# Norms that add the squares of a group on VectorE and multiply the sum once by ones on TensorE

## What is computed

```python
def rmsnorm(x, w):
    xf = x.astype(jnp.float32)
    y = xf * lax.rsqrt(jnp.mean(xf * xf, axis=-1, keepdims=True) + RMS_EPS)
    return (y * w.astype(jnp.float32)).astype(x.dtype)
```

## Time and profile before

| | |
|---|---|
| median of 3 runs | 3441.77 us |
| lowest and highest | 3435.27 and 3444.86 us |
| profiled execution, its own time | 3437.32 us |
| its span in the trace | 3435.5 us |
| TensorE, matmuls busy | 2918.2 us (85%) |
| VectorE busy | 2044.2 us (60%) |
| ScalarE busy | 882.5 us (26%) |
| GpSimd busy | 740.4 us (22%) |

### The profile page before, as it was taken

The page is one execution under the profiler, slowest core; times in us unless marked ns, Lnnn a source line. Parts: engine busy times, 40 slices in busy tenths (PEclk is TensorE's granted clock), DMA queues, the critical chain, the costliest instruction groups (busy, mean ns, idle before and its releaser), DMA issues. The chain is left out here.

```text
span 3435.5 us, 45234 instructions
## 1 busy us (share of the span) xinstructions
PE 2918.2 (85%) x15875; PEld 2538.4 (74%) x15875; DVE 2044.2 (60%) x3475; ACT 882.5 (26%) x1371; POOL 740.4 (22%) x501
## 2 busy tenths in 40 slices
PE   4888896989778699989898999999967865789987
PEld 2666674779566479988887999999965733568865
DVE  2777645334434337998867778888854255355532
ACT  1222112023111113433333333333321033133201
POOL 0333200000000005655453322222200000034400
PEclk7888898999889899999999999999988976899998
DMA  1111112211122225687879999999942100033230
GB/s 56 50 37 43 55 55 73 74 50 49 49 72 75 69 86 169 214 254 242 254 242 293 391 339 347 345 347 346 347 141 95 49 0 18 31 104 98 67 122 37
DMA packets 264492, 496.99 MB, mean 145 GB/s; under 512 B 118834, under 2 KB 171442, under 8 KB 262467
## 3 DMA queue, kind: packets, MB, share of 16 engines
q1 hardware_dynamic: 209090, 336.24, 29.6%
q0 software_dynamic: 36864, 134.23, 10.8%
q10 hardware_dynamic: 18432, 25.17, 2.0%
HBM read 443.14 MB, written 52.43 MB: 144 GB/s over the span
## 5 line engine op out<-in xcount | busy, mean ns | idle before, releaser
L238 PE MATMUL banks<-hb_high,experts_high 128*128 128x384 f32 x1024 | 363.6, 355 | 46.4 <-POOL experts_low L1403 34.4
L239 PE MATMUL banks<-hb_low,experts_high 128*128 128x384 f32 x1024 | 352.6, 344 | 0.0
L240 PE MATMUL banks<-hb_high,experts_low 128*128 128x384 f32 x1024 | 352.2, 344 | 0.0
L238 PE MATMUL banks<-experts_ah,experts_high 128*128 128x384 f32 x1024 | 343.1, 335 | 5.4 <-DVE experts_al L1568 5.4
L239 PE MATMUL banks<-experts_al,experts_high 128*128 128x384 f32 x1024 | 343.0, 335 | 0.0
L240 PE MATMUL banks<-experts_ah,experts_low 128*128 128x384 f32 x1024 | 343.0, 335 | 0.0
L1403 POOL TENSOR_TENSOR experts_low<-experts_raw,experts_high 128x1024 fp32r<-128x1024 f32 x94 | 227.3, 2419 | 344.5 <-ACT experts_high L1312 344.4
L238 PEld LDWEIGHTS banks<-hb_high,experts_high 128*128 128x128 f32 x1024 | 199.7, 195 | 52.7 <-POOL experts_low L1403 39.5
L1312 ACT ACTIVATE experts_high<-experts_raw 128x1024 fp32r<-128x1024 f32 x128 | 135.6, 1059 | 353.8 <-PE banks L240 238.3
L1370 ACT ACTIVATE experts_high<-experts_raw 128x1024 fp32r<-128x1024 f32 x128 | 135.7, 1060 | 340.3 <-PE banks L240 340.3
L1565 DVE TENSOR_TENSOR experts_low<-experts_raw,experts_high 128x1024 fp32r<-128x1024 f32 x128 | 156.9, 1225 | 102.8 <-ACT experts_high L1370 102.8
(11 more groups left out here) (489 smaller groups left out, 7087.2 us busy)
## 6 DMA issues: line engine op xcount, KB each, us to landing
experts_raw<-in_u SPq DMA_DIRECT2D x128, 512.0 KB, 5.6
experts_raw<-in_v SPq DMA_DIRECT2D x128, 512.0 KB, 5.8
early_experts<-experts_A ACTq DMA_DIRECT2D x128, 192.0 KB, 4.5
expert_weights<-shared SPq DMA_DIRECT2D x48, 512.0 KB, 8.2
shared<-expert_weights SPq DMA_DIRECT2D x128, 192.0 KB, 5.5
shared<-early_experts SPq DMA_DIRECT2D x128, 192.0 KB, 6.2
up_raw<-in_w_up SPq DMA_DIRECT2D x44, 512.0 KB, 3.4
ssd_raw_w<-in_w_xbc SPq DMA_DIRECT2D x26, 512.0 KB, 3.4
```

Of the source, the lines that this page charges most:

```text
L238: nc.tensor.matmul(to, w[0], x[0], start=start, stop=False)
L239: nc.tensor.matmul(to, w[0], x[1], start=False, stop=False)
L240: return nc.tensor.matmul(to, w[1], x[0], start=False, stop=stop)
```

## The change

```diff
-        sq = ctx.enter_context(nc.sbuf_tensor(f"{name}_sq", [P, 2, n], F32))
+        sq = ctx.enter_context(nc.sbuf_tensor(f"{name}_sq", [P, SLOTS, n], F32))
+        total = ctx.enter_context(nc.sbuf_tensor(f"{name}_total", [P, 2, n], F32))
...
-                        if m >= 2:
-                            act.wait_ge(square_used, m - 1)
-                        nc.scalar.activation(sq[:, m % 2, :], src[:, m, :], ACT.Square).then_inc(squared, 1)
-                    act.wait_ge(square_used, (g + 1) * tiles)
+                        if t == 0 and g >= 2:
+                            act.wait_ge(square_sum, g - 1)
+                        if t >= 1 and m >= SLOTS + 1:
+                            act.wait_ge(added, g * (tiles - 1) + t - SLOTS + (1 if t < SLOTS else 0))
+                        to = total[:, g % 2, :] if t == 0 else sq[:, m % SLOTS, :]
+                        nc.scalar.activation(to, src[:, m, :], ACT.Square).then_inc(squared, 1)
+                    act.wait_ge(square_sum, g + 1)
...
-                    for t in range(tiles):
-                        m = g * tiles + t
-                        pe.wait_ge(squared, m + 1)
-                        if t == 0 and g >= 2:
-                            pe.wait_ge(root, g - 1)
-                        for h in range(halves):
-                            last = nc.tensor.matmul(k.banks[:, 2 * (g % 2) + h, 0:w], ones,
-                                                    sq[:, m % 2, h * w:(h + 1) * w],
-                                                    start=(t == 0), stop=(t == tiles - 1))
-                        last.then_inc(square_used, 1)
+                    pe.wait_ge(added, (g + 1) * (tiles - 1))
+                    if g >= 2:
+                        pe.wait_ge(root, g - 1)
+                    for h in range(halves):
+                        last = nc.tensor.matmul(k.banks[:, 2 * (g % 2) + h, 0:w], ones, total[:, g % 2, h * w:(h + 1) * w],
+                                                start=True, stop=True)
+                    last.then_inc(square_sum, 1)
...
+                def add_squares(g):
+                    for t in range(1, tiles):
+                        dve.wait_ge(squared, g * tiles + t + 1)
+                        if t > 1:
+                            dve.wait_ge(added, g * (tiles - 1) + t - 1)
+                        nc.vector.tensor_tensor(total[:, g % 2, :], total[:, g % 2, :], sq[:, (g * tiles + t) % SLOTS, :], ALU.add
+                                                ).then_inc(added, 1)
+                add_squares(0)
                 for g in range(groups):
+                    if g + 1 < groups:
+                        add_squares(g + 1)
                     dve.wait_ge(root, g + 1)
```

More of the change, by code:

```diff
@@ L170, in norm_phase @@
     w = n // halves
-    squared, square_used, summed, root, recip, scaled = k.sems(name, "squared square_used summed root recip scaled")
+    squared, added, square_sum, summed, root, recip, scaled = k.sems(
+        name, "squared added square_sum summed root recip scaled")
+    SLOTS = 3
     with ExitStack() as ctx:
-        sq = ctx.enter_context(nc.sbuf_tensor(f"{name}_sq", [P, 2, n], F32))
+        sq = ctx.enter_context(nc.sbuf_tensor(f"{name}_sq", [P, SLOTS, n], F32))
+        total = ctx.enter_context(nc.sbuf_tensor(f"{name}_total", [P, 2, n], F32))
         std = ctx.enter_context(nc.sbuf_tensor(f"{name}_std", [P, 2, n], F32))
```

## The result

| | before | changed |
|---|---|---|
| median of 18 runs each, us | 3442.51 | 3454.09 |
| lowest and highest, us | 3432.75, 3448.07 | 3447.75, 3461.04 |
| profiled: span, us | 3435.5 | 3456.6 |
| profiled: mean granted clock | 0.914 | 0.897 |

The ratio is 1.0036, 95% interval 1.0027 to 1.0046. The changed kernel is some 12 us slower where I had forecast no change (3440.9 us), and its median lies above the range. The two profiled executions are 21 us apart, since the changed kernel's is 4 us slower than its median and the other 5 us faster: what the profiles show outside the norms is therefore more than what the medians have to explain.

The account below looks back on a forecast made before the run. Long norms were taken as bound by TensorE's multiplications up to the root, grouped norms mainly by VectorE. Terms -12.4 + 8.5 + 2.7 + 0.3 = -0.9 us, from 3441.8, gave 3440.9 us; range 3433 to 3448.

Parts of the forecast that it names:

- The long norms: Seven norms of one group: seven adds and one multiplication replace the multiplications by ones up to the root, -12.4 us.
- the gap between dependent adds: On VectorE, each add starts 0.04 us after its predecessor's end, so 0.73 us per add.
- Rival 1: Gap between dependent adds 0.15 us in place of 0.04: +5.9 us, 3446.8 us; chance 0.09.
- Rival 2: All 65 adds stretch by 0.53 us, as line 1973 does beside GpSimd: +34 us, 3475 us; chance 0.02.
- The lone multiplication: The one multiplication left per sum runs at the low clock: 2.16 us from its data to ScalarE's next start.
- ssd_n: Grouped norm: first reciprocal delayed 4.1 us by group 1's adds, later groups' adds 4.4 us; together +8.5 us.
- gla_n: Grouped norm, one add per group: reciprocal 1.3 us later, two more adds in VectorE's chain 1.4 us; together +2.7 us.
- Resets: Five more semaphores cleared at the three resets, at most 0.07 us each: +0.3 us.
- The step that failed: Outside the norms: 65 fewer TensorE multiplications are worth nothing more, and product phases start as cold as before.
- Rival 3: Longer TensorE idleness prolongs the cold start of the nine phases behind the norms: +23 us, 3464 us; chance 0.05.

Follow-up runs that it names:

- long_first: Change in the seven long norms only, plus five multiplications of constants ahead of TensorE's wait for the sum: 3428.04 us, ratio 0.9968 to the kernel before.
- before_sem: Kernel before with one unused semaphore more in each norm, allocated and cleared: 3439.22 us, ratio 0.9998.
- after_busy: Changed kernel plus, behind each lone multiplication, as many unread multiplications of constants as the change removed: 3443.43 us, ratio 1.0011 to the kernel before.
- fill_early: Changed kernel plus multiplications of constants behind the lone ones, only in ln1, ssd_n, gla_n and ln2: 3446.69 us, ratio 1.0013 to the kernel before.
- fill_first: Changed kernel plus the removed number of multiplications, of constants, in all norms ahead of TensorE's wait for the sum: 3441.35 us, ratio 1.0002 to the kernel before.
- long_warm: As long_first, plus eighteen multiplications of constants behind the sum in each long norm: 3466.13 us, ratio 1.0072 to the kernel before.
- after_again: Changed kernel timed once more, with a second trace: 3457.27 us, ratio 1.0038 to the kernel before.
- fill_late: Changed kernel plus multiplications of constants behind the lone ones, only in ln3 to ln7: 3456.33 us, ratio 1.0032 to the kernel before.
- before_pad34: Kernel before with 0.85 us of pure waiting on VectorE at the end of each of ln1, ssd_n, gla_n and ln2: ratio 1.0017.
- after_mid: Changed kernel with the next group's adds moved between reciprocal and scaling on VectorE: 3457.72 us, ratio 1.0046 to the kernel before.
- after_tiny: Changed kernel plus the same added multiplications as after_busy, each of one column only: 3446.55 us, ratio 1.0015 to the kernel before.
- after_pad: Changed kernel plus VectorE waiting of 2.3, 1.8, 1.2 and 1.0 us in ln1, ssd_n, gla_n and ln2: 3459.63 us, ratio 1.0058 to the kernel before.
- the three of the kernel before: Kernel before with VectorE delays: 1.7 us in ssd_n; 0.85 us in four norms; 8.4 in ssd_n and 2.2 in gla_n: ratios 1.0006, 1.0017, 1.0042.
- long_busy: Change in the seven long norms only, plus seven multiplications of constants behind each lone multiplication: 3431.35 us, ratio 0.9966 to the kernel before.
- long_only: Change in the seven long norms alone, ssd_n and gla_n as before: 3433.76 us, ratio 0.9984 to the kernel before.

## Why the prediction was wrong

**The long norms** (-12.4 us): mis-sized. They gave 9.6 us. The root came 8.82 us after the first square, not 8.42, and 7 times 0.4 us are the 2.8 us. The step that was off is the gap between dependent adds: I took 0.04 us from line 1973; seven adds of 692 ns in 5.47 us leave (5.47 - 7 x 0.692) / 6 = 0.104 us. Rival 1, with 0.15, was on the right side; why the gap is longer here than at line 1973 isn't shown. Rival 2 stayed away, as the adds take 0.69 us each; its condition holds in the trace of the kernel before, where 21 of the 22 adds of line 1973 run beside GpSimd and take 1.21 to 1.25 us, and the last, at 3266.0 us with GpSimd idle, takes 0.69. The lone multiplication was right: 2.17 us against 2.16. By the Trainium skill ("TensorE: Matmul & The Clock Gate", Part 1) it had to be a cold one, and the trace agrees; `long_first` shows the other price, 1.22 us from the last add to the root (2578.16 to 2579.38), when TensorE has been at work.

**ssd_n** (+8.5) and **gla_n** (+2.7) were right: 8.4 and 2.2 us, with the first reciprocal of `ssd_n` at 9.59 us (9.46 predicted). The close hit of the first owes something to the trace I started from: an execution of the old `ssd_n` at the lower clock takes 31.8 us, and against that the change costs 6.7. Adds ahead of a reciprocal whose squares stand behind the root on ScalarE: this is the costliest part of the change, and it is seen in the order of instructions alone. **Resets** (+0.3): nothing that `before_sem` can tell from zero.

With the sizes measured, the steps sum to +1.3 us in place of -0.9. The forecast would have been 3443, still 11 us below the 3454.1 measured.

**The step that failed** is that nothing outside the norms changes: "The 65 tile multiplications fewer on TensorE are worth nothing beyond the above". I had reasoned that nothing else ran on TensorE; but the edit also changes the clock that later work gets. Some 8 us of the 11 in the rest come back when multiplications are added off the path (`after_busy`, `fill_early`, `fill_first`), and the two traces of the changed kernel have the loss in the linear attention and the expert layer, not in the norms. The other 3 us are within the uncertainty of the ratios. Rival 3 had named the direction, a loss by TensorE's clock in phases whose code is the same, but not the mechanism: the phases right behind norms are not longer (the one behind `ln4`, 369.4 and 370.0 us), and `long_warm` shows that their start gains nothing when warm. It is to be counted as not confirmed.

**What carries the loss** is TensorE's clock. In the stretch from `ssd_n` to `gla_n`, which holds the linear attention and has the same code in all kernels, the traces differ by how often the clock falls to the low level for 13.7 us in which TensorE never pauses. Nine executions have no such fall and take 349.6 to 351.7 us; nine have one (352.4 to 355.9 us); `after_again` and `fill_late` have two (361.6 and 359.6 us). The two of `after_again`, columns as in the earlier trace rows:

```profile
761.20:774.90 13.70, 13.70 (x63) 12.95 (x63) 8.85 (x11) 6.76 (x12) 0.28 (x1) 0.50 0.00 0
850.00:863.70 13.70, 13.70 (x63) 12.95 (x63) 8.92 (x12) 6.96 (x12) 0.00 (x0) 0.50 0.00 0
```

Over all twenty traces, 1 us more at the low level in this stretch makes it 0.55 us longer (correlation 0.995). In the expert layer it is the same but looser, 0.65 us (0.87). `before_pad34`, with TensorE's program untouched, has a fall too (355.3 us), and `after_mid` has none, in an execution 10 us faster than its median. So falls come in both kinds of kernel and differ between executions of one kernel; that the changed kernel gets more of them on average is what the medians suggest, and one or two traces of each can't show it.

The Trainium skill ("TensorE: Matmul & The Clock Gate", HAM oscillation) reckons half of the throttled time as lost. The trace agrees where TensorE has no pause: 6.1 us for the fall at 757.9 us, which lasted 13.7 us. Over whole executions it is less. Each run lists its mean clock, and so its time at the low level, (1 - clock) x 2 x span; over 116 runs of the kernel before, a run with 1 us more at the low level is 0.33 us longer (correlation 0.78), over the changed kernel's 18 runs 0.37 us (0.74). One likely reason, not tested, is that part of the low time falls where TensorE only waits. Between kernels the sum doesn't tell: `after_tiny` has 693 us at the low level, the changed kernel 701, and they are 8 us apart. What counts is where the low clock falls.

**What stays open** is why it falls there. Neither the clock in the norms (`after_tiny`), nor program length (`fill_late`), nor the delays tried (`after_pad` and the three of the kernel before), nor TensorE's quiet (`long_warm`) explains all runs; the place of the later code in TensorE's program wasn't tested. The rest takes values from -1 to +13 us, and I can't say ahead of a run which one a kernel will have.

## What to carry to other kernels

An add per tile on VectorE is worth it where the engine waits anyway and there is one group; where groups are pipelined, look at what the adds stand ahead of on their own engine, and whose results they wait for. Where TensorE loses work, it is worth trying to give it some that nobody waits for: `long_busy`, with it behind the lone multiplication, is 12 us faster than the kernel before, `long_first`, with it ahead of the wait and short enough to end in time, 11, and `long_only`, without it, 6 (the intervals just touch). In `long_warm` too much of it cost some 32 us. And a forecast for a kernel of this length needs a term of some 5 to 10 us for what shifts of TensorE's clock do in phases that no edit touched; a sum of local terms that comes out within that is no evidence of "no change".

## What the runs showed of the hardware that I had not expected

- The clock falls in the middle of work: at 757.9 us of the changed kernel, with TensorE busy 13.25 of 15 us by small matmuls, and it costs 6.1 us. The same chain, run in the same rhythm, kept 1.00 in the kernel before, and a second execution of the changed kernel had two such falls.
- A chain of adds in which each waits for the one before takes 0.80 us per add of 128 x 512; the residual adds, independent of one another, start every 0.61 us ((2992.9 - 2988.6) / 7). The Trainium skill ("VectorE: DVE Perf Modes", The DRAIN you can't avoid) reports for a series of copies that a semaphore behind each costs nothing extra. The adds that wait for the one before are another case: they cost 0.19 us more each than the residual adds, which raise a semaphore each as well.
- With matmuls of one column in the norms the kernel is some 7 us faster elsewhere (1.0015 against 1.0036, intervals touching), at an unchanged clock of 0.50 in the norm.
